# Spare 128x256 products of constants in TensorE's waits, at some twenty places of a one-core kernel

## The chip, the core and the metric

The kernel runs on one core of one Trainium2 chip; the other seven are idle. The time is the device time of one execution in microseconds (us). Five engines work side by side and meet at semaphores: TensorE (matrix products, from SBUF into the eight banks of PSUM), VectorE and ScalarE (element-wise work, and everything that reads PSUM), GpSimd and SyncE (here almost only the queue of the DMAs). The profile calls them PE, DVE, ACT, POOL and SP. TensorE's clock is granted at one of two levels, 2.4 and 1.2 GHz; the profile writes it as a share, 1.00 and 0.50.

## What is computed

Two blocks of a model run one after the other over 256 tokens of 1024 channels, in float32. Cut to what matters:

```python
def first_block(x, c, ctx, ...):          # one layer
    mixed = _mixer(modulated ctx, modulated x, ...)   # mLSTM heads and RWKV-like heads, chunks of 64
    x = _layernorm(ALPHA * x + g1 * (mixed @ w_out), ...)
    ffn = _hier_moe(_modulate(x, sh2, sc2), ...)      # 32 experts, 1024 -> 512 -> 1024, two per group
    x = _layernorm(ALPHA * x + g2 * ffn, ...)
def second_block(x, c, ...):              # two layers
    x = x + g1 * mla_mixer(h)             # attention, 16 heads
    x = x + g2 * swiglu_ffn(h)            # 1024 -> 2816 -> 1024
    x = x + g1 * gdn_mixer(h)             # gated delta rule, 8 heads, 4 chunks of 64
    x = x + g2 * moe_ffn(h)               # 8 experts, 1024 -> 1408 -> 1024, two per token
    return rms_norm(x, final_norm)
```

Every block is modulated by vectors (`mod1`, `mod2`) that come from products of a conditioning vector with large matrices, the "ada" products.

## The kernel before

The state stays in SBUF, channels on the partitions: `xT` and `hT` are 8 tiles of 128 channels x 256 tokens. Weights (512 MB in all) stream from HBM through a ring of six slots in the buffer `work`; SyncE issues one load as soon as TensorE has used up what its slot held. The program is one list of instructions for each engine, written out by hand: there is no scheduler. TensorE's list is the order of the calls in the block under `@block.tensor` (L4161 to L4218), and an engine that meets a wait on a semaphore (`pe.wait_ge`) stops until the semaphore's count is reached; nothing behind it on that engine starts. So the order of the calls is the order of the work.

In this order come: the ada products and the transposes of the input (`ada_pe`, `ada_turn_pe`, L692), the projection `w_in_pe`, the mLSTM (`ml_tokens_pe`, `ml_keys_pe`, `ml_queries_pe`, `ml_step_pe`), the inversion of triangles for the RWKV heads (`rw_inverse_pe`, L1762 to L1819, with halves of ada products between its parts, `ada_halves_pe`, L641) and their eight steps (`rw_step_pe`, L1929 to L1978), the output projection, norms, the first experts (`route_pe`, `moe_pe("moe1")`), the attention (`mla_pe`, with `at_scores_pe` L3285 and L3291, `at_turn_pe` L3301 and `at_out_pe` L3311), its projection with norm 8 behind it, the dense layer (`ex_pe("ffn")`), norm 9, the delta rule (`gdn_pe`, `gd_chunk_pe`, L3645 to L3665, outputs turned at L3678), its projection, the second experts and the final norm.

A norm is sums over channels by TensorE (products with a matrix of ones: means L847, squares L855), squares by ScalarE (L904), the standard deviation by ScalarE (L916), its reciprocal by VectorE (L889), the scaling by VectorE (L894) and, where there is a bias, ScalarE (L923), which writes `hT` tile by tile.

The experts stand in a conditional: `moe_pe` asks whether the tokens of each expert fit the short way, and TensorE's list holds the short way and a long way behind it. Where the short way is taken, its end is an unconditional branch past the long way (L2922). Line 389 is the helper `product`, by which most projections go.

The lines that a fill stands against are waits such as these:

```python
4199        route_pe(w_rt1, 36, 3, "moe1")
4200        moe_pe("moe1")
4201        norm_rest_pe(4)
...
        pe.wait_ge(S["at_weights"], g + 1)     # at_turn_pe
        pe.wait_ge(S["gd_on"], c - 1)          # gd_chunk_pe, c = 2 and 3
```

Of the kernel before, what the change touches and what calls it, by code (L numbers as in the profile page):

```python
# [185 lines left out]
def build(nc, A, out, const_at):  # L186
# [205 lines left out]

    tok = [t.rearrange("p k n -> p (k n)").rearrange("p (t n) -> p t n", t=2) for t in (sq, xc)]
# [239 lines left out]
    def ada_halves_pe(n):  # L633

        pe.wait_ge(S["ada_evac"], n - 1)
        for q in range(2):
            h = 2 * (n - N_RW) + q
            half_landed(pe, h)
            w = half_unit(h)
            for j in range(4):  # L640
                ins = pe.matmul(ada_rows_at(n)[0][32 * j:32 * j + 32, :], cond[:, 4 * q + j, :], w[:, j, :],  # L641
                                start=q == 0, stop=q == 1)
            ins.then_inc(S["ada_half"], 1)
# [537 lines left out]
    def ml_tokens_pe():  # L1181

        pe.wait_ge(S["gate_exp"], 2)
        pe.wait_ge(S["ml_args"], 3)
        all_emptied(pe, "w_in")
# [3 lines left out]
        for g, (t, t0) in enumerate(((a_, N), (inter, 0), (einvm, 0))):  # L1189
            for c in range(4):  # L1190
# [3 lines left out]
                  stop=True).then_inc(S["ml_tok"], 1)  # L1194
        pe.wait_ge(S["zeroed"], 6)
# [119 lines left out]
    def ml_queries_pe():  # L1315

        pick = const("pick", R40).rearrange("p (r t) -> p r t", t=C)
        pe.wait_ge(S["ml_p"], 8)
        for d in range(2):
            if d:  # L1320
                pe.wait_ge(S["ml_args"], 3 + d)
            for p in range(4):
                ins = pe.matmul(PS[:, 2 + p // 2, (p % 2) * N:(p % 2 + 1) * N],
                                pick[gate_rows[d], d * H + 2 * p:d * H + 2 * p + 2, :].rearrange("p r t -> p (r t)"),
                                inter[gate_rows[d], :], start=True, stop=True)
            ins.then_inc(S["ml_ib"], 1)
# [423 lines left out]
    def rw_inverse_pe():  # L1750
        all_emptied(pe, "bonus")
        pe.wait_ge(S["hn_std"], 3)
        for d in range(2):
            pe.wait_ge(S["rw_ready"], d + 1)
            for g in range(4):
                if d:
                    pe.wait_ge(S["rw_ia"], 2 * g + 2)
                for i in (2 * g, 2 * g + 1):
                    t0 = ORDER[d][i] * P
                    for h in range(H):  # L1760
                        at = ((i % 2) * 4 + h // 2) * C
                        ins = pe.matmul(PS[half(h), 2 * g + h % 2, at:at + C], BK[half(h), d, h // 2, t0:t0 + C],  # L1762
                                        KR[half(h), d, h // 2, t0:t0 + C], start=True, stop=True)
                ins.then_inc(S["rw_nt"], 1)
# [15 lines left out]
        for n in range(N_RW, N_ADA1):  # L1780
# [3 lines left out]
            if n < N_RW + 4:  # L1784
                rw_first_tr_pe(n - N_RW)
        ada_turn_pe(N_ADA1 - 1)
        pe.wait_ge(S["rw_pre"], 3)
# [149 lines left out]
    def rw_step_pe(i):  # L1937
# [33 lines left out]
        if more:  # L1971
            pe.wait_ge(S["rw_bk"], i + 4)
            rw_sc_pe(i + 1, 1)
        pe.wait_ge(S["rw_ue"], 2 * (i + 1))
# [937 lines left out]
    def moe_pe(name):  # L2912

        gather_pe(name, 1) if name == "moe1" else ranked_gather_pe(0)
# [76 lines left out]
    def route_pe(w, cols_n, n_norm, name):  # L2991

        n_exp = COUNT[name]
        open_sums((2, 3))
# [216 lines left out]

    def mla_pe():
# [44 lines left out]
        all_emptied(pe, "kv")  # L3257
        pe.wait_ge(S["rope"], 2)
# [3 lines left out]
        for i in range(HP + 1):  # L3262
            if i < 4:
                ada_turn_pe(18 + i)
            if i + 2 < HP:
                at_scores_pe(i + 2)
            if i < HP:
# [367 lines left out]
    def gd_chunk_pe(c):  # L3635
        r, ro, cp, bank = half(c), gd_out_rows(c), c // 2, gd_out_bank(c)
        if c:
            if c == 1:
                pe.wait_ge(S["gd_ua"], 5)
            else:  # L3640
                pe.wait_ge(S["gd_on"], c - 1)
# [39 lines left out]
    def gdn_pe():  # L3681
# [50 lines left out]
        gd_inverse_pe(3)  # L3732
        all_emptied(pe, "gdn_z")
# [428 lines left out]
    def _(eng):  # L4162
# [13 lines left out]
        ada_pe(3)  # L4176
        ada_turn_pe(3)
        w_in_pe()
# [21 lines left out]
        moe_pe("moe1")  # L4200
        norm_rest_pe(4)
# [8 lines left out]
        out_pe("mla_out", oT, 8)  # L4210
        ex_pe("ffn")
        norm_pe(9)
        gdn_pe()
# [79 lines left out]
```

## Time and profile before

| | |
|---|---|
| median of 3 runs | 2133.8 us (2131.69 to 2136.89) |
| the profiled execution | 2135.58 us |
| its span, first to last instruction | 2133.6 us |
| TensorE busy | 1990.2 us, 93% |
| VectorE, ScalarE busy | 742.1 us, 414.1 us |
| mean granted TensorE clock | 0.955 |
| HBM traffic | 512 MB of DMA, mean 240 GB/s |

In a row of the profile, "L855 MATMUL PS<-sq,consts 128x256 x16" means sixteen records of line 855 that write the PSUM tensor from `sq` and `consts`. A float32 product of the program is recorded as two MATMULs (and two loads of weights), so these are eight products. "[3.46 <-ACT sq L904]" is the idle time of the engine before the first of them and what ended it.

### The profile page before, as it was taken

Reading aid. Unit: us, or ns where it says so; the run is one execution under the profiler, and the core shown is the slowest. Engines: PE = TensorE matmul, PEld = TensorE weight load, DVE = VectorE, ACT = ScalarE, POOL = GpSimd, SP = SyncE. Lnnn points to the kernel's source line nnn. Section 1 sums busy time; section 2 is a strip of 40 time slices with the busy share of each in tenths; the row PEclk is TensorE's granted clock in tenths of the full one; section 3 lists DMA queues with packets and bytes.
Section 4 is the critical chain, followed back from the end, with each engine's and each line's share of the span. In section 5 each row is a group of like instructions: output and inputs, shape, how many; then the busy total and the mean of one; then the engine's idle time right before and its main releaser. Section 6 shows DMA issues by size and latency. Waiting matters only on the chain.

```text
span 2133.6 us, 33687 instructions
## 1 busy us (share of the span) xinstructions
PE 1990.2 (93%) x14783; PEld 1338.4 (63%) x14783; DVE 742.1 (35%) x1592; ACT 414.1 (19%) x858; POOL 35.8 (2%) x36
## 2 busy tenths in 40 slices
PE   6999887899999999999898899999898899999998
PEld 3555666687554555544564688887777776463565
DVE  2683488564311111111324245324672420010002
ACT  3200244221311111111334200003232120000001
POOL 0000211000000000000000000000000000000000
PEclk9999887799999999999998999999999799999999
DMA  9610004106799999999755269753300049999991
GB/s 360 241 40 0 1 1 175 65 3 255 286 427 426 426 430 431 429 429 427 294 193 197 86 249 370 273 213 129 119 1 2 1 186 376 403 409 401 412 389 49
DMA packets 162046, 512.34 MB, mean 240 GB/s; under 512 B 9038, under 2 KB 32381, under 8 KB 149245
## 3 DMA queue, kind: packets, MB, share of 16 engines
q1 hardware_dynamic: 146432, 480.65, 57.2%
q10 hardware_dynamic: 15485, 29.77, 3.7%
q8 instruction: 105, 1.72, 0.3%
q14 instruction: 24, 0.20, 0.0%
HBM read 509.35 MB, written 1.05 MB: 239 GB/s over the span
## 4 chain that ended last, share of the span: by engine, by line
PE 86%; DVE 6%; DMA 4%; ACT 3%; issue 2%; SPq 0%; POOL 0%; ACTq 0%; DVEq 0%; POOLq 0%
PE PS L389 26%; PE PS L2536 10%; PE PS L2560 5%; PE PS L2372 4%; PE PS L2658 3%; PE PS L2451 3%; PE PS L2462 3%; PE PS L2650 2%; PE PS L2662 2%; PE PS L3209 1%; PE PS L855 1%; DMA work<-in_moe_w_gate_up_dram 1%; PE PS L2729 1%; PE PS L2089 1%; PE PS L682 1%
## 5 line engine op out<-in xcount | busy, mean ns | idle before, releaser
L389 PE MATMUL PS<-hT,work 128*128 128x256 f32 x1440 | 325.8, 386 | 4.5 <-ACT hT L923 4.0
L389 PEld LDWEIGHTS PS<-hT,work 128*128 128x128 f32 x1440 | 276.4, 193 | 49.9 <-issue 10.6
L2536 PE MATMUL PS<-work,sq 128*64 128x512 f32 x1024 | 222.6, 592 | 0.0
L389 PE MATMUL PS<-work 128*128 128x256 f32 (+1 forms) x608 | 194.6, 481 | 0.8 <-DVE work L4024 0.8
L2536 PEld LDWEIGHTS PS<-work,sq 128*64 128x64 f32 x1024 | 76.6, 137 | 143.2 <-issue 142.4
L389 PEld LDWEIGHTS PS<-work 128*128 128x128 f32 x608 | 117.2, 194 | 77.0 <-issue 65.7
L2560 PE MATMUL PS<-work 128*64 128x512 f32 x512 | 113.4, 595 | 10.0 <-issue 8.6
L2560 PEld LDWEIGHTS PS<-work 128*64 128x64 f32 x512 | 36.8, 137 | 76.3 <-issue 74.4
L2604 DVE TENSOR_TENSOR work<-work,PS 128x64 f32<-128x64 f32 x128 | 18.2, 215 | 184.9 <-PE PS L2536 184.9
L2650 PE MATMUL PS<-work,sq 128*64 128x512 f32 (+1 forms) x384 | 77.1, 558 | 5.8 <-DMA work<-in_moe_w_gate_up_dram 5.8
L2372 PE MATMUL PS<-work 128*128 128x256 f32 x352 | 76.3, 379 | 0.0
L2372 PEld LDWEIGHTS PS<-work 128*128 128x128 f32 x352 | 66.9, 190 | 9.1
L2451 PEld LDWEIGHTS PS<-work,xc 128*128 128x128 f32 x512 | 61.3, 200 | 12.2 <-issue 12.2
L2658 PE MATMUL PS<-work,sq 128*64 128x256 f32 (+1 forms) x576 | 66.0, 367 | 0.0
L2451 PE MATMUL PS<-work,xc 128*128 128x128 f32 x512 | 64.2, 286 | 0.0
L2130 DVE SCALAR_TENSOR_TENSOR xT<-PS,mod,xT 128x256 f32<-128x256 f32 x48 | 21.7, 481 | 121.1 <-PE PS L389 62.1
L2650 PEld LDWEIGHTS PS<-work,sq 128*64 128x64 f32 x384 | 29.1, 137 | 51.4 <-issue 44.1
L2517 DVE COPY work<-PS 128x1024 f32<-128x1024 f32 x16 | 19.6, 1225 | 117.1 <-PE PS L2560 117.1
L2462 PE MATMUL PS<-work 128*128 128x256 f32 x256 | 58.1, 380 | 1.4 <-DVE work L2517 1.4
L2580 ACT ACTIVATE work<-PS 128x64 f32<-128x64 f32 x128 | 16.6, 254 | 201.0 <-PE PS L2536 201.0
L2812 ACT ACTIVATE work<-PS 128x384 f32<-128x384 f32 (+4 forms) x24 | 9.8, 433 | 235.3 <-PE PS L2662 117.7
L2658 PEld LDWEIGHTS PS<-work,sq 128*64 128x64 f32 x576 | 42.7, 136 | 19.7 <-issue 4.3
(638 smaller groups left out, 2621.3 us busy)
## 6 DMA issues: line engine op xcount, KB each, us to landing
work<-in_ex_gate_dram SPq DMA_DIRECT2D x32, 2048.0 KB, 12.5
work<-in_ex_up_dram SPq DMA_DIRECT2D x32, 2048.0 KB, 15.5
work<-in_ex_down_dram SPq DMA_DIRECT2D x32, 2048.0 KB, 11.0
work<-in_moe_w_gate_up_dram SPq DMA_DIRECT2D x32, 2048.0 KB, 12.9
work<-in_moe_w_down_dram SPq DMA_DIRECT2D x16, 2048.0 KB, 16.9
work<-in_ada_w_dram ACTq DMA_DIRECT2D x14, 2048.0 KB, 11.2
work<-in_moe_w_gate_up_dram SPq DMA_DIRECT2D x16, 1536.0 KB, 14.9
work<-in_ada_w_dram SPq DMA_DIRECT2D x10, 2048.0 KB, 11.1
```

The lines of the kernel that those rows point to most:

```text
L389: ins = pe.matmul(outp, lhs, rhs, start=n == 0, stop=n == len(pairs) - 1, **kw)
L682: ins = pe.matmul(ada_rows_at(n)[0][32 * j:32 * j + 32, :], cond[:, 4 * q + j, :], w[:, 4 * q + j, :], start=q == 0, stop=q == 1)
L855: ins = pe.matmul(PS[:, banks[1], 0:N], ones, sq[:, k, :], start=k == 0, stop=k == kt - 1)
L2130: return dve.scalar_tensor_tensor(out=xT[:, m, :], in0=o, scalar=gate, in1=xT[:, m, :], op0=ALU.mult, op1=ALU.add)
L2372: ins = pe.matmul(PS[:, m // 2, (m % 2) * N:(m % 2 + 1) * N], wd[:, t, m * P:(m + 1) * P], hidden_of(k, t0 + t), start=opens and m % 2 == ...
L2451: ins = pe.matmul(PS[:, 4 + k // 4, (k % 4) * P:(k % 4 + 1) * P], htok[:, tt, k * P:(k + 1) * P], pickG[:, tt, :], start=tt == 0, stop=tt ...
L2462: ins = pe.matmul(PS[:, m // 2, (m % 2) * N:(m % 2 + 1) * N], ys[:, m * P:(m + 1) * P], spread, start=False, stop=closes, skip_group_check ...
L2536: ins = pe.matmul(PS[pair[m], 6 + j, :], xs[:, k, pair[m]], unit(U[name] + 3 * m + j, KT, F)[:, k, :], start=k == 0, stop=k == KT - 1)
L2560: ins = pe.matmul(PS[pair[m], 4 + j, :], hid[:, f, pair[m]], unit(U[name] + 3 * m + 2, FT, D)[:, f, j * 512:(j + 1) * 512], start=f == 0, ...
L2650: ins = pe.matmul(PS[pair2[m], bank, 0:n * P], xs[:, k, pair2[m]], w[m][:, k, :], start=k == 0, stop=k == KT - 1)
L2658: pe.matmul(PS[pair2[m], bank, 0:c1 - c0], xs[:, k, 0:C], w[0][:, k, c0:c1], start=k == 0, stop=k == KT - 1, skip_group_check=True)
L2662: ins = pe.matmul(PS[quarter[q], bank, 2 * P:DEEP_COLS], xs[:, k, C:DEEP], w[0][:, k, q * P:(q + 1) * P], start=False, stop=k == KT - 1, s ...
```

## The change

A helper `keep_busy(bank, n)` issues 2n products of the identity matrix (128x128) with 256 columns of the constants into a PSUM bank whose content nobody reads any more. It is called at 25 points of TensorE's list, with 170 products in all; nothing reads them, and no engine waits for them. Most calls stand right ahead of a wait. Some waits are put ahead of the fill or move up, so that the bank is free: the wait for `rw_pre` stands before the last half of the ada products, a wait for `ml_kw` before the second group of `ml_queries_pe`, one for `params` in the attention, and `all_emptied("w_in")` at the head of `ml_tokens_pe`. One of the two products that open the sums of the second experts (`open_sums`, L2310) moves from `route_pe` to the head of `moe_pe`.

```diff
+    def keep_busy(bank, n):
+
+        for _ in range(2 * n):
+            pe.matmul(PS[:, bank, 0:2 * P], ident, consts[:, 0:2 * P], start=True, stop=True, skip_group_check=True)
...
             h = 2 * (n - N_RW) + q
+            if n == N_ADA1 - 1:
+                if q:
+                    pe.wait_ge(S["rw_pre"], 3)
+                keep_busy(7 if q else 4 + n % 2, 2 if q else 3)
             half_landed(pe, h)
...
+        all_emptied(pe, "w_in")
+        keep_busy(4, 2)
         pe.wait_ge(S["gate_exp"], 2)
         pe.wait_ge(S["ml_args"], 3)
-        all_emptied(pe, "w_in")
...
                   stop=True).then_inc(S["ml_tok"], 1)
+        keep_busy(4, 2)
         pe.wait_ge(S["zeroed"], 6)
...
             if d:
+                pe.wait_ge(S["ml_kw"], NCH)
+                keep_busy(0, 5)
                 pe.wait_ge(S["ml_args"], 3 + d)
...
         all_emptied(pe, "bonus")
+        keep_busy(4, 3)
         pe.wait_ge(S["hn_std"], 3)
+        keep_busy(0, 5)
...
+        keep_busy(7, 1)
         ada_turn_pe(N_ADA1 - 1)
-        pe.wait_ge(S["rw_pre"], 3)
+        keep_busy(7, 2)
         pe.wait_ge(S["rw_id"], 7)
...
+        if not more:
+            keep_busy(6, 2)
         pe.wait_ge(S["rw_ue"], 2 * (i + 1))
...
+        if name == "moe2":
+            keep_busy(3, 4)
+            open_sums((3,))
         gather_pe(name, 1) if name == "moe1" else ranked_gather_pe(0)
...
-        open_sums((2, 3))
+        open_sums((2, 3) if name == "moe1" else (2,))
+        if name == "moe2":
+            keep_busy(3, 1)
...
+    ATTENTION_FILL = {5: 2, 6: 2, 7: 6}
...
         all_emptied(pe, "kv")
+        keep_busy(6, 1)
         pe.wait_ge(S["rope"], 2)
...
         for i in range(HP + 1):
+            if i < 2:
+                keep_busy(6, 2 - i)
             if i < 4:
                 ada_turn_pe(18 + i)
             if i + 2 < HP:
                 at_scores_pe(i + 2)
+            if i in ATTENTION_FILL:
+                pe.wait_ge(S["params"], 2 + ada_group(21))
+                keep_busy(7, ATTENTION_FILL[i])
             if i < HP:
                 at_turn_pe(i)
...
             else:
+                keep_busy(7, (5, 4)[c - 2])
                 pe.wait_ge(S["gd_on"], c - 1)
...
         gd_inverse_pe(3)
+        keep_busy(2, 5)
         all_emptied(pe, "gdn_z")
...
         ada_pe(3)
+        keep_busy(ADA_ROWS[0], 1)
         ada_turn_pe(3)
+        keep_busy(ADA_ROWS[0], 3)
         w_in_pe()
...
         moe_pe("moe1")
+        keep_busy(0, 7)
         norm_rest_pe(4)
...
         out_pe("mla_out", oT, 8)
+        keep_busy(6, 8)
         ex_pe("ffn")
         norm_pe(9)
+        keep_busy(0, 6)
         gdn_pe()
```

The first place is TensorE's list where the first experts end. Before, the last products of the means (L847) are followed by the branch past the long way, and behind it stand the products with the squares (L855):

```order
L2314 MATMUL PS<-consts 128x512 x4
L847 MATMUL PS<-xT,consts 128x256 x8
L2922 UNCONDITIONAL_BRANCH
L855 MATMUL PS<-sq,consts 128x256 x8
L682 MATMUL PS<-work,cond 32x512 x16
```

In the changed kernel the same lines are L856, L2943 and L864:

```order
L856 MATMUL PS<-xT,consts 128x256 x8
L2943 UNCONDITIONAL_BRANCH
L396 MATMUL PS<-consts 128x256 x14
L864 MATMUL PS<-sq,consts 128x256 x8
L691 MATMUL PS<-work,cond 32x512 x16
```

Fourteen spare products (L396) stand behind the branch and ahead of the squares' sums.

The second place is TensorE's list at the end of the attention. L3301 turns the weights of a pair of heads (`at_turn_pe`), L3311 forms its output (`at_out_pe`), L3285 and L3291 are the scores of a later pair. Before, from the scores of the last pair on:

```order
L3285 MATMUL PS<-work 128x128 x2
L3285 MATMUL PS<-work 128x256 x2
L3291 MATMUL PS<-work 128x128 x2
L3291 MATMUL PS<-work 128x256 x2
L3301 MATMUL PS<-consts,work 128x128 x6
L3311 MATMUL PS<-work 64x256 x2
L3311 MATMUL PS<-work 64x128 x2
L3301 MATMUL PS<-consts,work 128x128 x6
L3311 MATMUL PS<-work 64x256 x2
```

In the changed kernel, where the turn is L3332 and the output L3342:

```order
L396 MATMUL PS<-consts 128x256 x4
L3332 MATMUL PS<-consts,work 128x128 x6
L3342 MATMUL PS<-work 64x256 x2
L3342 MATMUL PS<-work 64x128 x2
L396 MATMUL PS<-consts 128x256 x4
L3332 MATMUL PS<-consts,work 128x128 x6
L3342 MATMUL PS<-work 64x256 x2
L3342 MATMUL PS<-work 64x128 x2
L396 MATMUL PS<-consts 128x256 x12
L3332 MATMUL PS<-consts,work 128x128 x6
```

Four products stand ahead of each of the turns 5 and 6, and twelve ahead of turn 7, the last.

The third place is the chunks of the delta rule: the products with the state (L3645), the outputs turned (L3678), the new state (L3660) and the part inside the chunk (L3665). Before, chunks 2 and 3:

```order
L3645 MATMUL PS<-work 128x128 x8
L3678 MATMUL PS<-consts,sq 128x64 x8
L3660 MATMUL PS<-xc,work 128x128 x8
L3665 MATMUL PS<-xc,work 64x128 x8
L3645 MATMUL PS<-work 128x128 x8
```

In the changed kernel, where L3677, L3710, L3692 and L3697 are the same lines:

```order
L3677 MATMUL PS<-work 128x128 x8
L3710 MATMUL PS<-consts,sq 128x64 x8
L3692 MATMUL PS<-xc,work 128x128 x8
L3697 MATMUL PS<-xc,work 64x128 x8
L396 MATMUL PS<-consts 128x256 x8
L3677 MATMUL PS<-work 128x128 x8
```

Eight products stand ahead of chunk 3, and, above these rows, ten ahead of chunk 2.

## Rows read from the trace of the kernel before

**Rows 1.** The page: granted clock in 40 slices, and the chain by engine.

```profile
PEclk9999887799999999999998999999999799999999
...
PE 86%; DVE 6%; DMA 4%; ACT 3%; issue 2%; SPq 0%; POOL 0%; ACTq 0%; DVEq 0%; POOLq 0%
```

**Rows 2.** Cores: span and mean granted TensorE clock.

```profile
core 0: 2133.6 us, clock 0.955
```

**Rows 3.** Chain of waits around the first experts' end: start us, us, what.

```profile
1032.73 3.47 PE PS L847 x16
...
1036.68 2.74 ACT sq L904 x8
...
1039.64 5.42 PE PS L855 x16
```

**Rows 4.** DMA queues at the same place: packets, MB, share of 16 engines.

```profile
q8 instruction: 1, 0.02, 0.8%
```

**Rows 5.** Chain of waits at the first norm of this kind, no branch ahead.

```profile
523.42 0.43 ACT sq L904
...
523.89 3.72 PE PS L855 x16
```

**Rows 6.** Stretches: length, busy by engine, granted clock (PEclk), DMA share, GB/s.

```profile
36.90:43.50 6.60, 4.47 (x12) 2.48 (x13) 4.67 (x16) 1.88 (x2) 0.50 (x3) 0.74 1.05 410
220.10:227.80 7.70, 5.60 (x35) 3.52 (x36) 1.77 (x5) 0.00 (x0) 3.26 (x2) 0.78 0.01 2
260.50:272.20 11.70, 9.57 (x34) 8.12 (x35) 6.55 (x12) 0.00 (x0) 1.82 (x1) 0.56 0.01 2
322.30:330.20 7.90, 2.96 (x56) 2.96 (x57) 7.90 (x9) 7.29 (x6) 0.00 (x0) 0.78 0.00 0
379.90:395.10 15.20, 10.57 (x117) 8.24 (x118) 9.13 (x23) 1.31 (x2) 2.77 (x2) 0.66 0.17 63
485.90:490.60 4.70, 3.53 (x69) 3.27 (x68) 1.77 (x5) 2.56 (x4) 0.00 (x0) 0.64 1.04 404
1036.20:1043.60 7.40, 3.95 (x11) 3.19 (x12) 2.74 (x8) 4.22 (x10) 0.00 (x0) 0.77 1.05 407
1124.30:1140.70 16.40, 13.92 (x94) 7.08 (x94) 8.70 (x19) 7.42 (x22) 0.00 (x0) 0.79 0.72 256
1149.40:1166.50 17.10, 16.13 (x88) 8.56 (x86) 6.12 (x15) 5.22 (x18) 0.00 (x0) 0.60 0.60 215
1215.20:1224.50 9.30, 5.27 (x13) 4.21 (x13) 5.01 (x9) 5.63 (x12) 0.00 (x0) 0.63 0.68 218
1462.10:1465.50 3.40, 0.01 (x2) 0.04 (x3) 2.94 (x4) 1.05 (x3) 0.00 (x0) 1.00 1.04 404
1634.80:1640.90 6.10, 3.95 (x36) 3.65 (x37) 3.85 (x4) 1.31 (x2) 0.00 (x0) 0.72 0.00 0
1656.60:1675.10 18.50, 16.00 (x79) 14.87 (x79) 10.55 (x14) 2.45 (x4) 0.00 (x0) 0.54 0.00 1
1731.70:1739.90 8.20, 5.53 (x27) 5.53 (x27) 4.61 (x25) 1.00 (x1) 0.00 (x0) 0.58 0.56 201
1780.00:2060.00 280.00, 271.19 (x2255) 148.40 (x2257) 20.65 (x40) 17.41 (x41) 0.00 (x0) 1.00 1.03 400
```

**Rows 7.** Timeline, end of the attention.

```profile
1171.86 0.88 PE L3301 MATMUL PS<-consts,work 128*128 128x128 f32 x6 [1.00 <-DVE work L3430]
...
1176.25 1.14 PE L3301 MATMUL PS<-consts,work 128*128 128x128 f32 x6 [2.71 <-DVE work L3430]
...
1177.32 1.55 PE L3311 MATMUL PS<-work 128*64 128x256 f32 x8
...
1178.79 1.50 PE L3301 MATMUL PS<-consts,work 128*128 128x128 f32 x6
...
1183.02 7.17 PE L389 MATMUL PS<-hT,work 128*128 128x256 f32 x32 [0.47 <-ACT hT L3364]
```

**Rows 8.** TensorE's longest wait in the second experts: total us, times, longest.

```profile
PE PS L2650 <- DMA work<-in_moe_w_gate_up_dram: 5.8, 5, 1.8
```

## The prediction

> **What bounds the kernel now.** I read the chain of waits first: 86% of it is TensorE [rows 1], so what TensorE's list loses, the kernel loses. Then the granted clock: its 40 slices show dips between the tenths 5 and 11, around 27, 31 and 33 [rows 1], and its mean of 0.955 over 2133.6 us [rows 2] means (1 - 0.955) x 2 x 2133.6 = 192 us at 1.2 GHz. Then stretches around each fill, each cut from the end of the work ahead of the fill to the end of the low clock behind it [rows 6]: length minus TensorE's busy time is the wait, and length x (1 - PEclk) x 2 is the low clock. The reader should see that the clock is low behind most of the waits, not in them.
>
> **What a fill costs.** Eight products of 128x256 took 3.47 us at 2.4 GHz, and eight took 5.42 us with 3.4 us of it at 1.2 GHz [rows 3]: 0.434 us for a product at the high clock, near twice that at the low one. The 170 products are 74 us of work. A fill that is shorter than its wait is free; a longer one makes everything behind it late by the rest.
>
> A page of the Trainium skill, "TensorE: Matmul & The Clock Gate", section "Back-to-back issue gap", gives 262 cycles at 2.4 GHz, 109 ns, for a product of 256 columns; it measured bf16, and the row shows four times that for this float32 form. By the page the 170 products would be an estimated 19 us, and no fill but one would outlast its wait.
>
> **The places, summed the same way.** For each: products x 0.434, less the wait, against half of TensorE's busy time in the low clock (its work there would take half). All from [rows 6], in us.
> - Ahead of the input projection (36.9): 8 products, 3.5; wait 2.1; late 1.3. Low 3.4, gives 1.7. Net gain 0.4.
> - mLSTM tokens (220.1): 8, 3.5; wait 2.1; late 1.4; gives 1.7. Gain 0.3.
> - mLSTM queries (260.5): 10, 4.3; wait 2.1; late 2.2. Low 10.3 less some 0.7 of wait in it, gives 4.8; but VectorE multiplies between the two groups of products and the next step, so I take 2.0 of the 2.6.
> - Inversion (322.3): 16, 6.9; wait 4.9; late 2.0. Low 3.4, 2.9 of it busy, gives 1.5. Loss 0.5.
> - Last ada halves (379.9): 16, 6.9; waits 4.6; late 2.3. Low 10.3, 9.1 busy, gives 4.5. Gain 2.2.
> - Last RWKV step (485.9): 4, 1.7; wait 1.2; low 3.4. Gain 1.1.
> - Attention, start (1124.3): 8, 3.5. The first two stand behind the wait that made TensorE idle, so only about 1.9 of the 2.5 idle can take them; late 1.6. Low 6.9, all busy, gives 3.4. Gain 1.8.
> - Dense layer (1215.2): 16, 6.9; wait 4.0; late 2.9. Low 6.9, 5.3 busy, gives 2.6. Loss 0.3.
> - Delta rule, start (1462.1): 12, 5.2; wait 3.4; and the clock is 1.00, so nothing is given back. Loss 1.8.
> - Solved triangles (1634.8): 10, 4.3; wait 2.2; late 2.2; gives 1.7. Loss 0.5.
> - Chunks 2 and 3 (1656.6): 18, 7.8; wait 2.5; late 5.3. Low 17.0, 15.9 busy, gives 8.0. Of the 2.7 I take 2.4, since VectorE's norm of the outputs stands between the chunks.
> - Second experts (1731.7): 8 and one moved product of 512 columns, 4.3; wait 2.7; late 1.7. Low 6.9, 5.5 busy, gives 2.8. The gain of 1.1 meets the weights: from 1780 to 2060 the DMA engines are full, 1.03 [rows 6], and TensorE already waited 5.8 us for them [rows 8]. I take 0.3; the two products in `route_pe` lie in a wait.
>
> Together 10.5 of gains less 3.1 of losses: 7.4 us faster. Two places are dearer than this.
>
> **End of the attention.** Turn 5 waited 1.00 us and turn 6 waited 2.71 us for VectorE, turn 7 for nothing: it began at 1178.79 where the output product of pair 5 ended [rows 7]. Four products (1.7 us) ahead of turn 5 make it 0.7 late; those ahead of turn 6 fit. So turn 6 begins at 1176.9, and at the high clock it and the output product take 0.9 each instead of 1.14 and 1.55: 1178.6. Then twelve products, 5.2 us, and the turn 0.9: 1184.7, against 1180.3 before. Behind it nothing is hidden: turn, evacuation, output, evacuation, projection follow each other, and the projection began at 1183.02. Loss 4.2, with the low clock here already paid back. The bounds: 0 if something unseen made turn 7 wait as long, 5.9 if the clock is no higher than before.
>
> **Behind the branch.** At 1036.2 TensorE stops, and the squares' sums begin at 1039.64. The chain names ScalarE's squares, which run from 1036.68 in 2.74 us for eight [rows 3]; but the first is done at 1037.1, and at the first norm the same line started 0.04 us after its first square (0.43 from 523.42, then 523.89) [rows 5]. So 2.5 of the 3.4 us are no wait for squares. What differs is the unconditional branch ahead, and in the wait one packet of 16 KB went over the instruction queue [rows 4]. I take it that TensorE waits for its instructions. The fill stands behind the branch, so it waits too: it begins at 1039.6, not at 1036.2. The clock falls as before, since TensorE did as little: 28 records, some ten of them until 1043.5 and eighteen at 0.217 us, end at 1047.4, and the sums end at 1050.9 instead of 1045.06. Loss 5.8. If the wait were for squares, the fill would begin at 1036.2, and 6.1 against 3.4 of wait, less 1.95 of low clock, would be a loss of 0.7.
>
> The Trainium skill, "Runtime: NRT & Kernel Launch", section "Instruction fetch mechanics", says that a taken branch to a target outside what is already fetched forces a DMA fetch before execution goes on. By that rule the loss is the 5.8 and not the 0.7, and the trace's packet agrees.
>
> **Sum.** 7.4 - 4.2 - 5.8 = -2.6: the profiled execution of 2135.6 becomes 2138.2. It stands 1.8 above the median of 2133.8, so the median becomes 2136.4.
>
> **Rivals.**
> - *Faster: the clock holds further, and the fill covers the branch.* Between 1149.4 and 1166.5 the attention has 13.7 us of low clock, all busy [rows 6], and no fill. It falls there behind short products and ada products, as at 1132; a fill upstream shifts them, and may keep it up. For: the gains are all on the chain. Against: nothing is added there. It gives 6.8, and a fill that covers the fetch gives 5.1: 2136.4 - 11.9 = 2124.5.
> - *Slower: the fills meet the low clock.* A product then takes 0.43 us more. Places where the clock was low when the fill would run: the end of the attention (low from 1176.7), the chunks, the branch; 52 products. If twenty of them run at 1.2 GHz beyond what I counted, and the work behind gets nothing back because its own clock rises no earlier, 8.7 us are added: 2145. It decides as soon as L396 takes over 0.6 us a product in these three places.
> - *Cheap products.* If a product of constants took a quarter of the rows' time, nothing would be late: all that the rows give back remains: the halves above and the branch's 2.0 add up to 36 us, of which VectorE and the weights keep some six; 2104. The section on the issue gap would have it so. Against: the same two records as in [rows 3]. Short fills may also not hold the clock.
> - *Nothing happens*: the fills fit because the waits grow, and the clock falls anyway; 2134.
>
> **How the numbers follow.** My forecast, 2136.4, has 0.45, with its own range of 2131 to 2142 (errors of 2 us at four large places, and the clock falls at other points in each execution). The faster rival 0.20, the slower 0.22, cheap products 0.05, nothing 0.08. A difference of 0.3%, 6.4 us, is what a measurement of this kernel tells from none: 2127.4 to 2140.2. A fifth of my forecast's chance lies above. So faster 0.26, same 0.43, slower 0.31. The range, 2124 to 2146, leaves out the cheap products and the ends.
>
> **What would show it.** In the changed profile L396 takes 0.43 us a product at the high clock; the squares' sums at the branch (L864) begin some 8 us behind the last L856, and the fill itself begins after about 3.4 us idle; the turn ahead of the attention's projection starts 5 us behind the output product; the clock stays at 1.00 in the ada halves, the chunks and the start of the attention; norm 9's fill is followed by products without a wait. The mean clock rises to about 0.97. I am wrong if the fills are shorter than 0.4 us a product, if the one behind the branch starts at once, or if TensorE's chain at the end of the attention holds a wait that the twelve products fill.

## The result: slower by half a per cent

The changed kernel took 2148.7 us (median of ten executions, 2137.0 to 2151.7) against 2135.8 for the kernel before (ten, 2128.1 to 2140.7): ratio 1.0047, 95% interval 1.0026 to 1.0069. (The ratio on record isn't the quotient of the two medians, which is 1.0060.) Seven more executions of it, run later beside the kernel before, gave 2145.3, ratio 1.0056 (1.0035 to 1.0077). All seventeen have a median of 2145.4; the 77 executions of the kernel before that ran beside the experiments have 2133.4. It is slower, in the middle by more than the 0.3% that I named as what can be told from no change, though the first interval begins at 0.26%. The forecast was 2136.4 in a range of 2124 to 2146. The recorded ratio times the 2133.8 that I started from is 2143.8, inside the range, as is the median of all seventeen; the median of the first ten lies 2.7 above its end. "Slower" had a chance of 0.31, "same" 0.43.

The profiled execution of the changed kernel is the shortest of the seventeen: 2136.98 us, 1.4 above the profiled one of before. So the pair of traces shows the steps, and the other executions have to say why the typical one is 12 us longer. First the two rows of the page, granted clock and chain by engine, as in [rows 1], and the core's span and clock, as in [rows 2].

```profile
PEclk9999997899999999999999999999999999999999
...
PE 87%; DVE 5%; DMA 4%; ACT 2%; issue 2%; SPq 0%; POOL 0%; ACTq 0%; DVEq 0%; POOLq 0%
```

```profile
core 0: 2135.0 us, clock 0.976
```

The mean clock rose from 0.955 to 0.976: (1 - 0.976) x 2 x 2135.0 = 102 us at 1.2 GHz instead of 192. The stretches of [rows 6] around the fills, in the changed kernel (length, busy by engine, PEclk, DMA share, GB/s):

```profile
256.70:268.90 12.20, 12.20 (x69) 10.10 (x68) 7.66 (x14) 0.00 (x0) 3.60 (x1) 1.00 0.00 1
378.80:393.30 14.50, 14.50 (x166) 11.15 (x167) 9.00 (x23) 1.55 (x3) 2.77 (x2) 1.00 0.20 72
1031.70:1047.00 15.30, 11.71 (x48) 9.62 (x52) 2.73 (x8) 4.44 (x11) 0.00 (x0) 0.89 1.05 404
1125.90:1140.90 15.00, 14.31 (x111) 8.53 (x111) 7.85 (x18) 7.51 (x22) 0.00 (x0) 1.00 0.81 279
1144.50:1161.70 17.20, 14.93 (x132) 8.54 (x132) 9.75 (x25) 8.49 (x27) 0.00 (x0) 1.00 0.86 306
1212.00:1223.50 11.50, 10.91 (x51) 9.29 (x50) 5.50 (x10) 6.76 (x13) 0.00 (x0) 1.00 0.59 173
1658.60:1677.10 18.50, 18.50 (x135) 16.74 (x133) 12.32 (x17) 2.45 (x4) 0.00 (x0) 1.00 0.00 1
```

Top to bottom: mLSTM queries, last ada halves, branch, the attention's start and its middle, dense layer, chunks 2 and 3. In all of them but the branch the clock is 1.00 where it was 0.54 to 0.79 before, and TensorE is busy for 87% to 100% of the time. The two places that the prediction called dear are next. The chain of waits at the branch (start us, us, what), which answers [rows 3]:

```profile
1028.19 3.45 PE PS L856 x16
1031.65 3.65 issue
1035.29 8.00 PE PS L396 x28
1043.29 3.47 PE PS L864 x16
```

The first sums end at 1031.64. Then TensorE stands for 3.65 us, for which the profile names no releaser, and only then does the fill start; 28 records take 8.00 us. One packet went over the instruction queue in that wait, as in [rows 4]:

```profile
q8 instruction: 1, 0.02, 0.7%
```

The squares' sums begin 11.6 us behind the end of the first sums, where they began 3.4 behind it before. The end of the attention, chain of waits, answers [rows 7]:

```profile
1172.76 0.80 PE PS L3342 x8
1173.56 5.38 PE PS L396 x24
1178.93 0.67 PE PS L3332 x6
...
1179.63 0.81 ACT work L3391
...
1180.97 0.89 PE PS L3342 x8
...
1182.31 2.86 PE PS L389 x12
```

Turn 7 (L3332 at 1178.93) stands behind 24 records of the fill, all on the chain. Twelve products took 5.38 us, 0.448 us each.

**Where the 1.4 us come from.** VectorE executes the same 1592 instructions in both kernels, so the start of each in the two traces, one less the other, gives how late the changed kernel is there. By the times of the trace before, it is 3.8 us early behind the ada halves (from 424), 4.5 early ahead of the branch, 1.7 late behind it, 4.4 early in the middle of the attention, 0.7 early behind its end, 0.8 late at the delta rule's start, 4.1 late ahead of the chunks, 0.5 late behind them, 1.4 late at the end.

### The profile page after: what moved, and what is told of

The parts are those of the page before. It is cut to its first block, busy times and chain, and to the rows that moved or that the text cites. A ratio compares the mean times of both kernels' runs of the same rounds, so it can differ in the third digit from the quotient of the medians.

```text
span 2135.0 us, 34363 instructions
## 1 busy us (share of the span) xinstructions
PE 2023.8 (95%) x15123; PEld 1370.5 (64%) x15123; DVE 742.1 (35%) x1592; ACT 413.8 (19%) x858; POOL 35.8 (2%) x36
## 4 chain that ended last, share of the span: by engine, by line
PE 87%; DVE 5%; DMA 4%; ACT 2%; issue 2%; SPq 0%; POOL 0%; ACTq 0%; DVEq 0%; POOLq 0%
PE PS L389 26%; PE PS L2554 10%; PE PS L2578 5%; PE PS L396 4%; PE PS L2390 4%; PE PS L2469 3%; PE PS L2676 3%; PE PS L2480 3%; PE PS L2668 2%; DMA work<-in_moe_w_gate_up_dram 2%; PE PS L2680 1%; PE PS L3232 1%; PE PS L2747 1%; PE PS L864 1%; PE PS L2107 1%
## 5 line engine op out<-in xcount | busy, mean ns | idle before, releaser
L396 PE MATMUL PS<-consts 128*128 128x256 f32 x340 | 83.0, 397 | 8.3 <-issue 3.6
L396 PEld LDWEIGHTS PS<-consts 128*128 128x128 f32 x340 | 65.2, 197 | 24.0 <-issue 12.7
## 6 DMA issues: line engine op xcount, KB each, us to landing
work<-in_ada_w_dram ACTq DMA_DIRECT2D x14, 2048.0 KB, 11.2
```

What stands on the lines that cost most here:

```text
L396: pe.matmul(PS[:, bank, 0:2 * P], ident, consts[:, 0:2 * P], start=True, stop=True, skip_group_check=True)
```

## The experiments

Each is compared with runs of the kernel before on the same chip. "Low" is (1 - clock) x 2 x span, averaged over the executions of a kernel.

```
kernel                              runs  median us  ratio (95%)               low us
before                                77  2133.4                                  186
changed (both sets)                   17  2145.4     1.0047, 1.0056               122
no fill behind the branch             12  2139.3     1.0020 (1.0005 to 1.0036)    124
none ahead of turn 7                  12  2142.9     1.0049 (1.0031 to 1.0068)    125
without four dear fills               12  2134.1     0.9999 (0.9982 to 1.0016)    127
every fill halved                      6  2119.9     0.9928 (0.9904 to 0.9952)    121
every fill a quarter                  12  2128.8     0.9967 (0.9949 to 0.9985)    154
moves alone, no products              12  2136.7     1.0011 (0.9992 to 1.0030)    189
before + branch fill                   7  2146.0     1.0049 (1.0031 to 1.0066)    207
before + the fill ahead of the branch 12  2140.0     1.0026 (1.0013 to 1.0040)    191
before, fallback's body first         12  2137.3     1.0022 (1.0006 to 1.0037)    198
halved, two out                        6  2110.9     0.9887 (0.9859 to 0.9916)    122
halved, two out, one swap              5  2107.9     0.9885 (0.9865 to 0.9905)    115
```

**1. The changed kernel again.** No edit.

> The changed kernel once more, for another execution's trace. Of its ten executions nine were longer than the profiled one (2136.98 us), most by 7 to 15 us, at granted clocks of 0.967 to 0.974 against 0.976. My theory: what the fills add (some 40 us beyond their waits) is the same in every execution, what the clock gives back is not. Then this execution, if it is long, has about 125 us of low clock instead of 102, each us of it costing near half a microsecond, and the losses behind the branch (6 us) and ahead of turn 7 (4 us) stand unchanged. Rival: the extra time is in a wait that has grown (weights, VectorE); then the low clock is the same and one of the longest waits is longer by 5 us or more. Median: 2148.7 as before.

Measured: 2145.3; the profiled execution 2145.2 at a clock of 0.971. Its low clock is 2143.3 x 0.029 x 2 = 124 us, 22 more than in the first trace, and it is 8.2 us longer. The branch is 7.3 us late in it and the end of the attention 3.7, as in the first, and no wait for the second experts' weights grew. But one place turned about: over the last ada halves this execution loses 3.3 us, where the first gained 2.4. The timeline there (start us, us, engine line, operation, in brackets the idle time ahead and its releaser):

```profile
374.84 1.06 PE L650 MATMUL PS<-work,cond 128*32 128x512 f32 x8 [0.58 <-DMA work<-in_w_ada_dram]
378.78 1.94 PE L650 MATMUL PS<-work,cond 128*32 128x512 f32 x8 [2.87 <-DMA work<-in_w_ada_dram]
380.64 1.87 PE L701 MATMUL PS<-consts,w_g 128*128 128x2 f32 x8
382.37 4.37 PE L396 MATMUL PS<-consts 128*128 128x256 f32 x12
386.67 1.06 PE L650 MATMUL PS<-hT,cond 128*32 128x512 f32 x8
```

The same products in the first trace of the changed kernel:

```profile
375.01 1.94 PE L650 MATMUL PS<-work,cond 128*32 128x512 f32 x8 [0.30 <-DMA work<-in_w_ada_dram]
377.33 1.06 PE L650 MATMUL PS<-work,cond 128*32 128x512 f32 x8 [0.39 <-DMA work<-in_w_ada_dram]
378.33 1.05 PE L701 MATMUL PS<-consts,w_g 128*128 128x2 f32 x8
379.24 2.84 PE L396 MATMUL PS<-consts 128*128 128x256 f32 x12
```

The last two halves in the kernel before, whose waits the prediction summed:

```profile
380.63 1.06 PE L641 MATMUL PS<-hT,cond 128*32 128x512 f32 x8 [0.71 <-DMA hT<-in_w_ada_dram]
384.43 1.60 PE L641 MATMUL PS<-work,cond 128*32 128x512 f32 x8 [2.73 <-DMA work<-in_w_ada_dram]
```

A half of an ada block has to wait for its weights. In the second trace the 2.87 us of that wait stand ahead of the fill, at an earlier half than where the fill was put, and the fill then runs at 1.2 GHz: 4.37 us for what took 2.84. The low clock and the two losses are what my theory said. But 5.7 of the 8.2 us lie over these halves, so part of the extra time is a wait that changed place, which neither of my theories had.

**2. Without the fill behind the branch.**

```
         moe_pe("moe1")
-        keep_busy(0, 7)
```

> The changed kernel without the 14 products behind the first experts' branch. Theory (TensorE waits for instructions there, and the fill waits with it): 6 us faster than the changed kernel, 2142.7. Rival (the 3.4 us are a wait for squares, the fill lies in it): 0.7 us faster, 2148. Rival (the fill holds the clock for what follows): slower than the changed kernel by 1 or 2 us.

Measured: 2139.3, 6.1 us under the changed kernel's 2145.4. In its trace the stretch with the branch costs 0.3 us less than before, against 6.2, 7.3 and 7.4 in three traces with the fill. The rival of 0.7 is out.

**3. Every fill halved.**

```
-        for _ in range(2 * n):
+        for _ in range(n):
```

> The changed kernel with every fill cut to half, 85 products, 37 us. By the waits of the kernel before, only four places are then late: turn 7 by 2.6, the branch by 3.0, the chunks by 1.4, the solved triangles by nothing; 7 us in all against 40. If the clock gives back half of what it gave the profiled execution (38 us), it is 12 us faster than the kernel before, 2124. Rival (short fills hold the clock as well as long ones): 2107. Rival (fills that leave part of a wait idle hold nothing): 7 us slower than before, 2143.

Measured: 2119.9, 25 us under the changed kernel and 14 under the kernel before. Its low clock is 121 us: the halved fills hold the clock just as well as whole ones, and of the 37 us of products that went 25 were on the path. The rival of 2107 had the low clock right and the time 13 us off, the forecast of 2124 was 4 off: as much low clock is gone as with whole fills, but with the 7 us late of the expectation the clock gave back only some 21 us (13.5 + 7), near the 19 that the forecast took.

**4. Without four dear fills** (branch, turn 7, dense layer, start of the delta rule).

```
-    ATTENTION_FILL = {5: 2, 6: 2, 7: 6}
+    ATTENTION_FILL = {5: 2, 6: 2}
...
         moe_pe("moe1")
-        keep_busy(0, 7)
...
-        keep_busy(6, 8)
         ex_pe("ffn")
         norm_pe(9)
-        keep_busy(0, 6)
```

> The changed kernel without the fills at four places at which the pair of traces shows a loss: behind the branch (6.0), ahead of turn 7 (4.1), ahead of the dense layer (1.1) and of the delta rule (1.4). If the places add up: 12.6 us faster than the changed kernel, 2136, level with the kernel before. Rival (these fills also hold the clock further on in most executions): 6 us faster only, 2143.

Measured: 2134.1, 11.3 under the changed kernel; low clock 127 against 122. The places add up, within the noise of some 4 us, and the kernel is level with the one before: at this length the remaining fills together gain nothing that can be told.

**5. The branch's fill alone,** on the kernel before.

```
         moe_pe("moe1")
+        keep_busy(0, 7)
```

> The kernel before with one fill alone, the 14 products behind the first experts' branch (6.1 us at the high clock). Theory (the fill waits 3.5 us for instructions, as the sums did, and then runs in front of them): 6 us slower than the kernel before, 2141, by up to 8 where the low clock meets the fill. The pairs of traces so far bore out 6.2 and 7.3. Rival (the wait is for squares): 1 us slower, 2136.

Measured: 2146.0, 12 us slower, twice what I expected. At its own place the profiled execution loses 7.5 us; the chain of waits there:

```profile
1031.72 3.45 PE PS L852 x16
1035.17 3.69 issue
1038.86 9.24 PE PS L396 x28
1048.10 1.94 PE PS L860 x9
```

The fill takes 9.24 us, since two thirds of it run at 1.2 GHz: the clock falls for the wait ahead of it. The other 5 us lie at places that this edit doesn't touch, and the low clock is 207 us in the mean of seven executions against 187 on the same chip. Why it should be more is open.

**6. The same fill ahead of the branch.**

```
             norm_first_pe(n, k)
+        if name == "moe1":
+            keep_busy(0, 7)
```

> The same 14 products, ahead of the branch: behind the first sums of the norm, inside the body that the branch leaves. Theory A (instructions behind the branch are fetched only when the products ahead of it are nearly done): the wait of 3.5 us stands behind the fill, and the kernel is 5 to 6 us slower than before, 2141. Theory B (the fetch runs beside the fill): the sums follow the fill without a wait; 6.1 less 3.5 us, less 1 to 2 of low clock: 1 us slower, 2136. Under B with the wait gone in the trace, but the wait of squares as its cause, the time would be the same; the kernel with the fallback's body first tells these apart.

Measured: 2140.0, 6.5 us slower. The chain of waits:

```profile
1034.27 3.45 PE PS L852 x16
1037.72 6.04 PE PS L396 x28
1043.76 1.92 issue
1045.68 3.73 PE PS L860 x16
```

Between the two theories in the wait, which shrinks from 3.7 to 1.92 us, so part of it now lies beside the fill; the place loses 2.8 us. The squares ran from 1038.2 to 1040.9, beside the fill, so the 1.92 are no wait for them. The other 3.7 us of the 6.5 aren't at this place, and what they are is open. The packet of the instruction queue shows when the fetch runs. In the kernel before it starts at 1037.26, 1.06 us after TensorE's last sum, and TensorE goes on 2.38 us after its start. In the first trace of the changed kernel these are 1.2 and 2.44 us. Here the packet starts at 1043.29, 0.47 us before the fill ends and not beside its beginning, and TensorE goes on 2.39 us later.

**7. The body that isn't run stands first,** on the kernel before, for TensorE alone.

```
+        with pe.If(ok == 0):
+            weight_rows_pe(name)
+            ex_pe(name)
+            norm_behind_pe(name)
         with pe.If(ok == 1):
             ex_pairs_pe(name) if name == "moe1" else ex_ranked_pe()
             norm_behind_pe(name)
-        with pe.If(ok == 0):
...
```

> The kernel before, no fill. On TensorE the two conditional bodies of the experts change places, so that the body that isn't run stands ahead of the one that is: the jump over it comes before the experts' work, and behind their work nothing is skipped. Theory (the 2.5 to 3.5 us at the end of the first experts are the instructions' fetch behind the jump over the unused body): that wait shrinks to the 0.8 us that the squares take, and the clock falls less; 3 to 4 us faster, if the jump at the start lies beside another wait; if it costs as much there, no change. Rival (squares): the sums behind the experts start 3.4 us behind the last sum, as before; no change there at all. Forecast 2133.

The timeline at the end of the first experts, and at the start of the second:

```profile
1033.92 3.62 PE L847 MATMUL PS<-xT,consts 128*128 128x256 f32 x16
1038.51 3.72 PE L855 MATMUL PS<-sq,consts 128*128 128x256 f32 x16 [0.97 <-ACT sq L904]
...
1730.01 1.88 PE L2310 MATMUL PS<-consts 128*128 128x512 f32 x4
1733.99 16.20 PE L389 MATMUL PS<-sq,work 128*128 128x128 f32 x143 [2.10 <-issue]
```

In the kernel before, the second of these groups followed the first at once:

```profile
1742.40 7.87 PE L389 MATMUL PS<-sq,work 128*128 128x128 f32 x69
```

With nothing skipped behind the experts, the wait is 0.97 us, and it is for the squares; the place is 4.2 us faster in the trace. With the second fallback now skipped ahead of the second experts, 2.10 us appear there that weren't there before, and the instruction queue's packet starts 2.69 us before TensorE goes on. So the wait of [rows 3] is the fetch behind a jump over a body that isn't run, and it goes where the jump goes. The Trainium skill's "Runtime: NRT & Kernel Launch", section "Instruction fetch mechanics", has a taken branch outside what is fetched wait for a DMA; both places agree with it, at 2.1 and, less the squares' own wait, 2.5 us. The median, though, is 2137.3, not under the kernel before, with a low clock of 198 us against 187 on the same chip. Of the 4.2 us, 2.2 come back ahead of the second experts, and the other 2 are less than the spread between executions. That nothing of them is left in the median is open, as in 5.

**8. Halved, without the fills at the branch and at turn 7.** The edits of 3 and of 2, and the first of 4.

> The changed kernel with every fill halved, and without the fills behind the branch and ahead of turn 7. Halved fills alone gave 2119.9. By the waits, these two are 3.0 and 2.6 us late and give the clock little: 2114.5. Rival (what they hold of the clock is worth as much as they cost): 2120.

Measured: 2110.9, with 122 us of low clock: 1.1% faster than the kernel before. The median is 9 us under that of 3, against 5.6 by the waits; the two ratios differ by 0.41%, known to some 0.37% either way, so the 9 can't be told from the 5.6.

**9. The changed kernel without turn 7's fill.** The first edit of 4.

> The changed kernel without the 12 products ahead of turn 7 of the attention. Theory (nothing waits there, 5.2 us of products of which the clock pays one back): 4.2 us faster than the changed kernel, whose 17 executions so far have a median of 2145.4: 2141.2, and in the trace the projection starts where turn 7's output has been evacuated. Rival (TensorE's work before the projection has slack, the fill is free): no change. Rival (the fill holds the clock of the projection and the norm behind it): slower by 1 or 2 us.

Measured: 2142.9, 2.5 us less than the changed kernel's 2145.4, each known to some 4 us either way: by the time alone it can't be told from 4.2, nor from nothing. The trace tells it. The chain of waits:

```profile
1176.97 1.04 DVE work L3461 x2
...
1178.06 0.89 PE PS L3332 x6
...
1180.31 0.89 PE PS L3342 x8
...
1181.65 1.56 PE PS L389 x6
```

Here the output product of pair 5 began at 1176.83 and the projection at 1181.65, 4.8 us behind it; in the changed kernel it was 1172.69 and 1182.31, 9.6 us. In the three traces with this fill the stretch is 3.7 us late against before, in the two without it 1.1 early. The difference is 4.8.

**10. Every fill at a quarter,** `range((n + 1) // 2)`: 49 products.

> The changed kernel with every fill at a quarter, rounded up: 49 products, 21 us. Halves gave 2119.9 with as little low clock (121 us, mean of six) as whole fills (122 us, mean of seventeen; the kernel before 187). Theory A (what holds the clock is that the wait is not idle from end to end; a short fill does): low clock near 125 us and only turn 7 and the branch late, by 1.3 and 1.7: 2109. Theory B (a fill has to take most of its wait): low clock of 150 us or more, 2120 or above. Forecast 2116.

Measured: 2128.8, low clock 154 us. Theory B in the clock and in the time: these fills leave half of the waits idle, and only half as much low clock goes as with the longer ones (32 us against 64). Of the lengths tried, none, 49, 85 and 170 products, 85 is the best; nothing between them was run.

**11. The moves without products,** `range(0)`.

> The changed kernel with no products in its fills: what is left is what it moves (the wait for the keys' products ahead of the mLSTM queries, the waits for the parameters and for the decayed keys put earlier, two sums opened apart). If the moves cost nothing, as the prediction has it: the kernel before, 2134 and 187 us of low clock. Rival (the moved waits hold TensorE up): slower by 2 us or more.

Measured: 2136.7, ratio 1.0011 (0.9992 to 1.0030), low clock 189 us. No difference that can be told; the interval reaches 6 us, so the rival's 2 us aren't excluded by it. In this kernel's trace, though, the last ada halves read otherwise than in the one that I had predicted from:

```profile
384.61 1.94 PE L650 MATMUL PS<-work,cond 128*32 128x512 f32 x8 [3.02 <-DMA work<-in_w_ada_dram]
386.48 1.87 PE L701 MATMUL PS<-consts,w_g 128*128 128x2 f32 x8
388.28 1.93 PE L650 MATMUL PS<-hT,cond 128*32 128x512 f32 x8
389.99 1.65 PE L650 MATMUL PS<-work,cond 128*32 128x512 f32 x8
...
395.22 4.98 PE L1808 MATMUL PS<-consts,sq 64*32 64x64 f32 x124 [1.71 <-DVE sq L1904]
```

The last two halves, around which the fill is put, wait for nothing; what waited 3.02 us is the half before them. Of the 4.6 us of waits only 1.71 are left for 6.9 us of products.

**12. The best of these:** edits of 8, and the first experts' fallback ahead of the body that is run; the second experts keep their order.

> Halved fills, none behind the branch nor ahead of turn 7 (2110.9), and TensorE's two bodies in other order for the first experts alone: the one that isn't run stands first. In the kernel with the swap at both places the wait at the end of the first experts fell from 3.4 to 0.97 us, and 2.1 us appeared at the start of the second ones. So 2.4 us and some low clock: 2107.5. Rival (its median was no lower than that of the kernel before, though the wait was gone: the clock takes it back elsewhere): 2111.

Measured: 2107.9, ratio 0.9885 (0.9865 to 0.9905), low clock 115 us. It has the lowest median of all, 1.1% under the kernel before, but it can't be told from the 2110.9 without the swap. In its trace the place is 4.2 us faster than before, as in 7.

## Why the prediction was wrong in size

The forecast had the direction, and the time lies in its range, but the sum put the change at +2.6 us, and it is +12 between the medians. The two dear places were read rightly, and they decide the sign. What failed is the sum of the other places, and in it above all what the clock was to give back. The profiles give the net of each: how much later the stretch makes the kernel in the traces with whole fills, less the same in the traces without (the kernel before and those of 5, 6, 7 and 11; a trace from which a place's fill was taken out counts as without there; at the branch those of 5, 6 and 7 don't count as without, and 5 counts as with). The last column is the mean of the three kernels with halved fills, less the same. "Last RWKV step" runs on to the branch, and "second experts" to the end of the kernel. Plus is time lost.

```
place                        predicted  traces: with less without   halved fills
start, mLSTM tokens               -0.7   -1.2                        -3.5
mLSTM queries                     -2.0   -3.6                        -3.4
inversion                         +0.5   +1.1                        -0.2
last ada halves                   -2.2   +2.1                        -3.6
last RWKV step                    -1.1   -1.1                        +0.2
branch                            +5.8   +7.2                        (one: +3.3)
attention, start and middle       -1.8   -0.5                        -1.5
end of the attention              +4.2   +4.1                        (one: +1.6)
dense layer                       +0.3    0.0                        -3.1
delta rule, start                 +1.8   +0.7                        -0.7
delta rule, 1472 to 1605           0     +0.8                        -1.2
solved triangles                  +0.5   +0.2                        -2.9
chunks 2 and 3                    -2.4   -2.1                        -4.5
second experts                    -0.3   -0.7                        -0.7
```

These are means over three to five traces with and four to seven without, and single traces differ by 3 to 8 us at the queries, the ada halves and the attention. The first column adds up to +2.6, the second to +7. The profiled executions with whole fills happen to be 2.3 us shorter in the mean than the medians of their kernels, so the traces don't carry all of the 12; some 2 to 3 us stay open.

- **The price of a product** was right: 0.448 us at the high clock at turn 7, 0.57 behind the branch, where 3.4 of 8.00 us were at the low one. The 109 ns of the Trainium skill's "TensorE: Matmul & The Clock Gate", section "Back-to-back issue gap", which was the rival of cheap products, isn't the price of this float32 form: it takes four times that.
- **Behind the branch** was right in its mechanism: the fill starts after 3.65 us, the sums 11.6 us behind the first sums. The term was 1.4 us too small: I let eighteen of the records run at the high clock, and in three of four traces some 5.8 of the fill's 9.1 us were at the low one. The sign that I gave, sums "some 8 us behind", didn't follow from my own working, which has 11.2; measured are 11.6.
- **The end of the attention** was right to 0.6 us: 4.8 for the twelve products by the pair with and without, 4.1 net of all. My own times, 1184.7 less 1180.3, make 4.4 and not 4.2.
- **The ada halves are the place that failed most,** by 4.3 us in the means. "16, 6.9; waits 4.6; late 2.3" took the waits of one execution for the waits of the kernel. The weights' wait moves between the halves from one execution to the next, and the fill stands at two of them. In the kernel without products 1.7 us of wait were left there. The five traces with fills scatter here from 2.6 us gained to 3.1 lost.
- **The mLSTM queries** belong to this. In three of the five traces without fills (5, 7 and 11) the clock was low for 23.9 us from 260 on, and not for the 10.2 of the trace that I read. Those three lose 5.4 us more at the queries and win 2.7 back at the ada halves. Queries, inversion and ada halves together were to gain 3.7 us and gain 0.4.
- **"Gives" is the step that failed.** Each place was given half of its busy time in the low clock back. With the two dear places the sum takes some 35 us given back, against 37 late. The low clock went nearly as counted: 75 us at the twelve places, and over all executions it is 186 less 122, 64. What was too high is what a microsecond of it is worth. With the 37 late, a kernel that is 12 us slower got back 25; with halved fills, 7 late and 13.5 faster, it got back 21. That is 0.32 to 0.39 us for each of the 64. The first two traces of the changed kernel say the same, 8.2 us for 22 us of low clock, and so do the executions of one kernel among themselves: a line through time against low clock, for all thirteen kernels together, rises by 0.29. So 10 to 14 of the 35 us were missing, and the error of the sum is 9.4. These are estimates that lean on my list of what is late, and why a microsecond is worth less than a half is open. In the first trace of the changed kernel the longest dips that stay begin at 339, 404, 1537 and 1681, where there is no fill; in the second two are where a fill stands, at the ada halves and at the branch, after the clock had fallen ahead of it.
- **Attention, middle.** The clock held from 1144 to 1161 in the first trace, as the faster rival had it, for 4.6 us; in the second it fell at 1153 again. Without any fill it held there in the trace of 7 too, but for 3.4 us, so the gain of the first trace isn't shown to be the fills'.
- **The slower rival** named the right time, 2145, by another way: it wanted over 0.6 us a product at the end of the attention, in the chunks and behind the branch, and the first two were at the high clock in both traces of the changed kernel. Behind the branch three of four traces had 0.65 us a product.
- **Delta rule's start, dense layer, solved triangles, chunks, second experts** are within 1.1 us of what was said in the means.

Halving shows what the changed kernel does wrong. Its fills were longer than their waits by some 37 us in my own list (25.2 at the twelve places, 5.9 and 6.1 at the dear ones), and I set that against the low clock without asking whether a shorter fill would hold the clock as well. It does: 121 us of low clock with 85 products, 122 with 170.

## What to carry to other kernels

Where short idle waits make the clock fall, spare products in them can pay, but size each to no more than its wait. At the twelve places the waits add up to 34 us. Whole fills were 1.7 times that and made the kernel 0.5% slower, halved fills 0.86 of it and made it 0.7% faster at the same granted clock, and fills of half the waits lost half of what the clock had gained. Don't put them behind a jump or where the engine has stopped waiting; first see, in more than one trace, that the wait is at that instruction in each. A gain that comes from the clock has to be read from the mean clock of many executions, since one profiled execution can be the best of seventeen.

## What the runs showed of the hardware

- A jump over a body that isn't run cost TensorE 3.4 to 3.8 us at the end of the first experts and 2.1 at the start of the second, with one 16 KB packet on the instruction queue that starts 2.4 to 2.7 us before TensorE goes on. Products ahead of the jump cover about half of it. With the body that isn't run put first, the wait at the first experts' start was 0.64 us in one trace and 1.14 in another, against 2.5 saved at their end.
- An edit at one place moves the low clock elsewhere. One fill at 1036 raised the mean low clock of the whole kernel from 187 to 207 us (seven executions), and the change of the bodies, which takes a wait away at the same place, to 198 (twelve, with 16 us of spread between them). With a spread of 4 us between executions of one kernel, an edit of 3 us is told from nothing only where its own place in the trace is read.
